# The end of a transformer kernel: the last tile of the last output product, the final norm and the stores in halves of columns

## What is computed

```python
def swiglu_layer(x, g, w_gate, w_up, w_down):      # the last layer, in short
    h = rms_norm_2(x, g)
    return x + (silu(h @ w_gate) * (h @ w_up)) @ w_down

def rms_norm_2(x, g):
    xf = x.astype(jnp.float32)
    y = xf * lax.rsqrt(jnp.mean(xf * xf, axis=-1, keepdims=True) + NORM_EPS)
    return (y * g.astype(jnp.float32)).astype(x.dtype)

...
    return rms_norm_2(x, final_norm)
```

## Time and profile before

| | before |
|---|---|
| three runs | 3154.92, 3155.46, 3160.68 us (median 3155.46) |
| profiled execution: its time | 3158.48 us |
| profiled execution: span of the trace | 3156.6 us, mean granted TensorE clock 0.991 |
| instructions | 44657 |
| PE busy | 3040.8 us (96%) |
| POOL busy | 2161.4 us (68%) |
| DVE busy | 1291.8 us (41%) |
| ACT busy | 729.7 us (23%) |

### The profile page before, as it was taken

One profiled execution on the slowest core, in us unless ns is written; L12 is line 12 of the kernel. 1 busy time (PEld: TensorE's weight loads), 2 busy tenths in 40 slices (PEclk: granted clock), 3 DMA queues, 4 the chain that ended last, 5 costly groups with the idle time before them and its releaser, 6 DMA issues.

```text
span 3156.6 us, 44657 instructions
## 1 busy us (share of the span) xinstructions
PE 3040.8 (96%) x14210; PEld 2409.9 (76%) x14210; DVE 1291.8 (41%) x2257; ACT 729.7 (23%) x1486; POOL 2161.4 (68%) x3010
## 2 busy tenths in 40 slices
PE   7999999999989999999999799899999999999998
PEld 5667888888767688888887577688887777778886
DVE  5653343222455533543235665522225554441223
ACT  4422111010333211210012544410002443320101
POOL 7456777787864577787887355487778444677875
PEclk9999999999999999999999899999999999999999
DMA  4122223222321222222223121122222112222222
GB/s 178 54 68 87 94 95 112 94 97 96 106 100 62 74 94 100 90 100 95 98 100 110 43 68 64 61 94 93 100 94 99 61 54 74 87 87 100 94 100 87
DMA packets 78366, 281.33 MB, mean 89 GB/s; under 512 B 8576, under 2 KB 9088, under 8 KB 77440
## 3 DMA queue, kind: packets, MB, share of 16 engines
q1 hardware_dynamic: 74752, 265.74, 25.1%
q10 hardware_dynamic: 3456, 13.50, 1.2%
HBM read 277.11 MB, written 2.10 MB: 88 GB/s over the span
## 4 chain that ended last, share of the span: by engine, by line
PE 87%; DVE 7%; ACT 3%; issue 1%; DMA 0%; DVEq 0%; POOL 0%; SPq 0%; ACTq 0%; POOLq 0%
PE pa L680 42%; PE pd L680 37%; PE pd L938 2%; PE po L966 2%; ACT work L192 1%; PE pa L946 1%; PE pd L758 1%; DVE h_lo L204 1%; DVE work L200 1%; ACT h_hi L192 1%; DVE po L196 1%; PE pa L723 1%; DVE x_res L196 1%; PE pd L987 1%; DVE qk L204 1%
## 5 line engine op out<-in xcount | busy, mean ns | idle before, releaser
L634 POOL TENSOR_TENSOR w_lo<-w_raw,w_hi 128x256 fp32r<-128x256 f32 x2004 | 1535.9, 797 | 41.8
L629 POOL TENSOR_SCALAR w_hi<-w_raw 128x512 fp32r<-128x512 f32 x1002 | 626.9, 644 | 926.3 <-PE pa L680 557.2
L680 PE MATMUL pa<-h_hi,w_hi 128*128 128x512 f32 (+1 forms) x1944 | 781.6, 402 | 25.1 <-POOL w_lo L634 20.4
L680 PE MATMUL pa<-h_hi,w_lo 128*128 128x512 f32 (+1 forms) x1944 | 752.7, 387 | 0.0
L680 PE MATMUL pa<-h_lo,w_hi 128*128 128x512 f32 (+1 forms) x1944 | 752.4, 387 | 0.0
L680 PEld LDWEIGHTS pa<-h_hi,w_hi 128*128 128x128 f32 x1944 | 366.6, 189 | 136.0 <-issue 55.7
L680 PEld LDWEIGHTS pa<-h_lo,w_hi 128*128 128x128 f32 x1944 | 366.9, 189 | 81.9 <-issue 11.3
L680 PEld LDWEIGHTS pa<-h_hi,w_lo 128*128 128x128 f32 x1944 | 366.4, 188 | 75.5
L680 PE MATMUL pd<-b_hi,w_hi 128*128 128x512 f32 x992 | 389.5, 393 | 6.5 <-DVE x_res L196 2.6
L680 PE MATMUL pd<-b_hi,w_lo 128*128 128x512 f32 x992 | 386.9, 390 | 0.0
L680 PE MATMUL pd<-b_lo,w_hi 128*128 128x512 f32 x992 | 386.9, 390 | 0.0
(11 more groups left out here) (200 smaller groups left out, 3181.0 us busy)
## 6 DMA issues: line engine op xcount, KB each, us to landing
w_raw<-in_w SPq DMA_DIRECT2D x501, 512.0 KB, 3.2
mrg<-in_nabias ACTq DMA_DIRECT2D x2, 2048.0 KB, 9.0
mrg<-in_mem ACTq DMA_DIRECT2D x3, 1024.0 KB, 4.8
x_res<-in_x SPq DMA_DIRECT2D x8, 256.0 KB, 4.9
out_y<-mrg ACTq DMA_DIRECT2D x8, 256.0 KB, 2.1
vbuf<-in_count ACTq DMA_DIRECT2D x2, 512.0 KB, 4.2
qk<-in_mem ACTq DMA_DIRECT2D x1, 1024.0 KB, 7.8
b_all<-in_delta ACTq DMA_DIRECT2D x2, 448.0 KB, 4.0
```

The lines of the kernel that those rows point to most:

```text
L629: ins = nc.gpsimd.tensor_scalar(w_hi[:, j, half], raw[:, j % RR, half], 1.0, 1.0, ALU.mult, ALU.mult)
L634: ins = nc.gpsimd.tensor_tensor(w_lo[:, j, part], raw[:, j % RR, part], w_hi[:, j, part].bitcast(F32), ALU.subtract)
L680: ins = mm(out, a, b, start=(first and k == 0 and e == 0), stop=(last and k == k_n - 1 and e == 2))
```

## The change

The last group's output product gets functions of its own, `last_residual` on PE, ACT and DVE. Tiles 0 to 6 are made as before in 512 columns, written out instead of looped over. Tile 7 is made in two halves of 256 columns, each in a bank of its own, and all that follows goes by these halves: addition, square, product with ones (`last_sum`), logarithm, exponential, square, the two root steps, scaling and stores. The sum of the first half stands in PE's list before the last two of the second half's six steps. ACT multiplies tiles 0 to 2 by the gain ahead of time (`gained`), POOL multiplies these by `rx`, DVE scales tiles 3 to 7. SP stores the first halves of all tiles and the second halves of POOL's, ACT the second halves of DVE's.

```diff
@@ @block.sync
+            def store(k, h, scaled, count):
+                sp.wait_ge(scaled, count)
+                sp.dma_start(dram["out"][k][:, HALVES[h]], mrg[:, k, HALVES[h]]).then_inc(out_first, 16)
+
+            for at in range(KT - POOLED):
+                store(POOLED + at, 0, last_root, 2 + at)
+            for k in range(POOLED):
+                store(k, 0, by_pool, 1 + k)
+            for k in range(POOLED):
+                store(k, 1, by_pool, 1 + POOLED + k)
+            sp.wait_ge(out_first, 16 * (KT + POOLED))
@@ @block.gpsimd
+            pool.wait_ge(gained, POOLED)
+            for h, half in enumerate(HALVES):
+                pool.wait_ge(last_root, 1 + h * (1 + KT - POOLED))
+                for k in range(POOLED):
+                    nc.gpsimd.tensor_tensor(mrg[:, k, half], mrg[:, k, half], rx[:, half], ALU.mult).then_inc(by_pool, 1)
@@ @block.tensor
+            def last_residual(k_n):
+
+                pe.wait_ge(split_full, n.last("split_full"))
+                for m in range(KT - 1):
+                    linear(bank_d(), B, k_n).then_inc(cdone, 1)
+                s = next_chunk()
+                for h, half in enumerate(HALVES):
+                    bank = bank_d()
+
+                    def waits(k):
+                        if h and k == k_n - 2:
+                            last_sum(0)
+                    ins = products(bank[:, 0:S // 2], [w_tile(s, k) for k in range(k_n)],
+                                   [act_tile(B, k, half) for k in range(k_n)], waits=waits)
+                    if h:
+                        ins.then_inc(cdone, 1)
+                    else:
+                        n.take("pd_full")
+                        ins.then_inc(pd_full, 1)
+                last_sum(1)
+
+            def last_sum(h):
+                bank, half = bank_a(), HALVES[h]
+                if h == 0:
+                    pe.wait_ge(acc_part, n.at("acc_part", n.n["acc_part"] + KT - 2))
+                mm(bank[:, 0:S // 2], ones, acc[:, half], start=True, stop=False)
+                pe.wait_ge(last_squared, h + 1)
+                mm(bank[:, 0:S // 2], ones, pair2[:, 1, half], start=False, stop=True).then_inc(last_summed, 1)
...
-                    residual(B, g, ends and not last)
                     if ends and last:
-                        for _ in range(KT):
-                            n.take("acc_part")
+                        last_residual(g)
+                    else:
+                        residual(B, g, ends)
...
-            stream_norm(True)
@@ @block.scalar
+            def last_residual():
+                for m in range(KT - 1):
+                    n.take("x_full")
+                    prepare(m)
+                    if m < POOLED:
+                        f(mrg[:, m], x[:, m], ACT.Copy, scale=col("final", m)).then_inc(gained, 1)
+                act.wait_ge(acc_part, n.free("acc_part", n.n["acc_part"], 2))
+                for h, half in enumerate(HALVES):
+                    act.wait_ge(last_added, h + 1)
+                    f(pair2[:, 1, half], x[:, KT - 1, half], ACT.Square).then_inc(last_squared, 1)
+                    act.wait_ge(last_summed, h + 1)
+                    mean_square = pa[n.take("pa_done") % RA][:, 0:S // 2]
+                    chain(f(rx[:, half], mean_square, ACT.Ln, scale=1.0 / D))
+                    chain(f(rx[:, half], rx[:, half], ACT.Exp, scale=-0.5))
+                    f(pair2[:, 1, half], rx[:, half], ACT.Square).then_inc(last_rooted, 1)
...
-            stream_norm()
-            for k in range(KT):
-                act.wait_ge(t_full, n.at("t_full", n.take("t_full")))
-                act.dma_start(dram["out"][k], mrg[:, k]).then_inc(out_in, 16)
-            act.wait_ge(out_in, 16 * KT)
+            for at in range(KT - POOLED):
+                k = POOLED + at
+                act.wait_ge(last_root, 1 + KT - POOLED + 2 + at)
+                act.dma_start(dram["out"][k][:, HALVES[1]], mrg[:, k, HALVES[1]]).then_inc(out_in, 16)
+            act.wait_ge(out_in, 16 * (KT - POOLED))
@@ @block.vector
+            def last_residual():
+                clear_sum()
+                for m in range(KT - 1):
+                    add_x(m)
+                    prepare(m, "final", False)
+                for h, half in enumerate(HALVES):
+                    if h:
+                        n.take("cdone")
+                    d = full_d(h == 1)
+                    v.tensor_tensor(x[:, KT - 1, half], x[:, KT - 1, half], pd[d % RD][:, 0:S // 2], ALU.add)\
+                        .then_inc(last_added, 1)
+                dve.wait_ge(last_added, 2)
+                for h, half in enumerate(HALVES):
+                    mean_square = pa[n.take("pa_done") % RA][:, 0:S // 2]
+                    dve.wait_ge(last_rooted, h + 1)
+                    chain(v.scalar_tensor_tensor(pair2[:, 0, half], mean_square, -0.5 / D, pair2[:, 1, half],
+                                                 ALU.mult, ALU.mult))
+                    v.scalar_tensor_tensor(rx[:, half], pair2[:, 0, half], 1.5, rx[:, half], ALU.add, ALU.mult)\
+                        .then_inc(last_root, 1)
+                    dve.wait_ge(last_root, 1 + h * (1 + KT - POOLED))
+                    for k in range(POOLED, KT):
+                        scaled(mrg[:, k, half], x[:, k, half], col("final", k), rx[:, half]).then_inc(last_root, 1)
...
-            stream_norm()
-            for k in range(KT):
-                n.take("t_full")
-                scaled(mrg[:, k], x[:, k], col("final", k), rx[:, :]).then_inc(t_full, 1)
```

More of the change, by code:

```diff
@@ L555, in build @@
         set_up = sem("set_up")
+        last_added, last_squared = sem("last_tile_added"), sem("last_tile_squared")
+        last_summed, last_rooted, last_root = sem("last_half_summed"), sem("last_half_rooted"), sem("last_root")
+        gained, by_pool = sem("gained"), sem("scaled_by_pool")
+        out_first = sem("first_halves_stored")
+        HALVES = (slice(0, S // 2), slice(S // 2, S))
+        POOLED = 3
         block = ctx.enter_context(nc.Block())
@@ L1538, in residual, with ffn @@
                     prepare(m, name)
-            def ffn(next_name=None, between=None):
+            def last_residual():
[13 more added lines that the diff above has]
+                    f(pair2[:, 1, half], rx[:, half], ACT.Square).then_inc(last_rooted, 1)
+            def ffn(next_name=None, between=None, last=False):
                 stream_norm()
@@ L1559, in ffn @@
                         log_and_exp()
-                    residual(ends, next_name)
+                    if ends and last:
+                        last_residual()
+                    else:
+                        residual(ends, next_name)
             def gates(l):
@@ L1689, in cross_and_ffn @@
                 half_residual(f"b{l}_ffn")
-                ffn(None if l else "b1_mix")
+                ffn(None if l else "b1_mix", last=l == 1)
             load(tabs[:], dram["tabs"][:, 0:512], aux_in[5])
@@ L2171, in add_x, with residual @@
                 v.give(x_full)
-            def residual(name=None, split=True):
+            def last_residual():
[20 more added lines that the diff above has]
+                        scaled(mrg[:, k, half], x[:, k, half], col("final", k), rx[:, half]).then_inc(last_root, 1)
+            def residual(name=None):
                 if name:
@@ L2177, in residual @@
                         add_x(m)
-                        prepare(m, name, split)
+                        prepare(m, name)
                     return
@@ L2222, in ffn @@
                         between(number)
-                    residual(next_name if number == len(GROUPS) - 1 else None, next_name != "final")
+                    if number == len(GROUPS) - 1 and next_name == "final":
+                        last_residual()
+                    else:
+                        residual(next_name if number == len(GROUPS) - 1 else None)
             def gates(l):
```

## The result

| | before | after |
|---|---|---|
| median (22 executions each) | 3156.44 us | 3161.57 us |
| lowest to highest | 3154.92 to 3160.68 | 3158.77 to 3164.20 |
| profiled execution: time / span | 3158.48 / 3156.6 us | 3161.30 / 3159.5 us |
| mean granted TensorE clock | 0.991 | 0.989 |

The ratio after by before is 1.0015, with a 95% interval of [1.0009, 1.0022], +5.1 us in the medians. That is within 0.2%, but the interval leaves no change out: the kernel is a little slower. In microseconds it goes from +2.8 to +6.9. The forecast was +3.1 us and 3158.6 us, its range ended at 3162.3.

The account below looks back on a forecast made before the run. PE was taken to bound the kernel, with a 14.95 us serial tail behind its last product. Base 3155.46 us plus 3.4 (late start), plus 1.6 (clock), less 1.85 (tail), +3.1 in all, gave 3158.6 us; range 3155.0 to 3162.3.

Parts of the forecast that it names:

- late start of tile 0: Start of the last output product: tile 0 waits for all six hidden tiles, so its sixth step comes later, +3.4 us.
- low clock behind the stand: Behind PE's 3.85 us stand ahead of tile 0: one 3.4 us stretch at clock 0.50, +1.6 us, bounds 0 and 5.
- writing the loop out: Tiles 0 to 6 of the last output product: same 126 matmuls at the same pace, no cost.
- tail in halves: From tile 7 to the end: halves scaled on two engines end at 3154.75 instead of 3156.6, -1.85 us.
- Rival (2): Behind the stand ahead of tile 0: the clock stays up or falls while PE still stands, 3157.0 us; chance 0.2.
- Rival (3): Scalings in the tail: no collision on SBUF, both engines at their own pace, 1.8 us less, 3156.8 us; chance 0.1.
- Rival (4): Last output product: the late start costs nothing, only the shorter tail shows, 3153.6 us; chance 0.06.
- rival (5): Behind the stand ahead of tile 0: the low clock stays, costing 5 us, 3162.0 us; chance 0.1.
- 3.45 us for a half: Tail: POOL's three scalings take 2.5 us, DVE makes 3.15 tiles meanwhile and 1.85 alone in 0.95.
- scalings at 0.7 to 0.8 us each: Sign in the changed kernel's profile: DVE's `mrg` scalings take this long beside POOL's.
- The store: End of the tail: last store taken as 2.44 us as before; an estimate of 0.3 us shorter was left out.

Follow-up runs that it names:

- e3_fill: The changed kernel with 15 filler matmuls, results unused, ahead of its late wait: 3159.34 us, ratio to before 1.0009.
- e1_early: The changed kernel with the waits of before at tile 0, the last hidden tile awaited only ahead of the sixth step: 3156.58 us, ratio to before 1.0000.
- e2_wait: The kernel before, with only the last output product's wait for all six hidden tiles moved ahead of tile 0: 3162.11 us, ratio to before 1.0017.
- e6_root_psum: e1_early, but ACT copies the root into PSUM and DVE reads it there from its second tile on: 3153.61 us, ratio to before 0.9992.
- e4_dve_all: e1_early with DVE scaling all eight tiles in halves and POOL none: 3155.45 us, ratio to before 0.9997.
- e5: e1_early with POOL scaling four tiles instead of three and DVE four: 3155.61 us, ratio to before 0.9993.
- e7_gain_ahead: e6_root_psum with ACT multiplying seven tiles by the gain ahead of time instead of three: 3153.96 us, ratio to before 0.9990.
- e8_fill6: e3_fill with 6 filler matmuls instead of 15 ahead of the late wait, one execution: 3158.18 us.

## Why the prediction was right, and where its sum was off

The forecast was +3.1 us, within 0.2%, by a late tile 0 and one stretch of low clock, less a shorter tail. All three parts are there, and the sign is right. Of the parts:

| term | forecast | measured |
|---|---|---|
| late start of tile 0 | +3.4 | +3.41 (e3_fill against e1_early) |
| low clock behind the stand | +1.6 | +1.6 (changed kernel against e3_fill; e2_wait) |
| writing the loop out | 0 | 0 (e1_early: 25.29 us as before) |
| tail in halves | -1.85 | -1.1 |
| sum | +3.1 | +3.9 by the traces, +5.1 by the medians |

The measured median, 3161.57, lies 3.0 us above the forecast 3158.6 and only 0.7 below the end of the range. One microsecond of the three is the base: the forecast started from the median of three runs, 3155.46, and that of 22 is 3156.44. The tail's term makes 0.8, and 1.2 are open (below). That the range held is in part luck, since its upper end was set for a clock that stays low, which did not happen. Two slips in the working change nothing that matters: the two root steps of 0.43 us end at 3144.26 by the sum, not at 3144.32, and (2) less the 1.8 us of (3) is 3155.2, not 3155.0.

**The wait.** It was read from one row, the 0.45 us stand ahead of the sixth step: five steps lay in front of a wait that was always going to be waited for, and moving them behind it costs their full length, because PE has no later stand that could take it up. Rival (4), that the late start costs nothing, is refuted by e2_wait.

**The clock.** The value between the two bounds, 0 and 5 us, was the right one: one stretch at the low level, then back. Rival (2) would have given 3112.20 to 3115.50 at 1.00, as e3_fill has it, and rival (5) a clock that stays down past 3115.6. The two neighbours that it was placed between, stands of 3.27 and 4.21 us, were a good guide: in all eleven traces the clock is low behind these two (0.50 to 0.68 in the 3.3 us that follow). The third, the stand of 2.34 us that kept the clock and carried rival (2), was a poor one: in two of the eleven traces, that of the changed kernel among them, the clock falls behind it too (last section).

**The tail.** Here a size was off, the term "3.45 us for a half". The path of the first half up to the first scaling was forecast at 3144.42 - 3137.40 = 7.02 us and took 3148.58 - 3141.37 = 7.21 (+0.2). The five scalings took 3.81 and 3.73 us instead of 3.45 twice (+0.64), the step from one series to the next 3153.58 - 3152.39 = 1.19 instead of 0.99 (+0.2), and the last store 2.2 instead of 2.44 (-0.25). These give +0.8, the difference between -1.85 and -1.1. The greatest part is the collision: beside POOL DVE needs 0.84 us and 1.05 for the first, not the 0.79 of the earlier trace rows, and what POOL holds up is three DVE instructions, 2.8 us, as the third goes on when POOL's 2.5 us have ended. The sign that the prediction gave, scalings at 0.7 to 0.8 us each, was so far too low. Rival (3), no collision, is refuted, and it names what could be had: e6_root_psum takes most of the collision away and wins 0.9 us.

**The store.** The prediction left out that a half tile's store is shorter. It is, by some 0.25 us (2.2 against 2.44). The estimate that the prediction worked out from the Trainium skill, "DMA: Bandwidth & Descriptors", section "Anatomy of one DMA — SWDGE (gpsimd) path", was 0.3 less; the trace comes near it, though the page's figures are for transfers that GpSimd issues, and these are issued by ACT and SP.

**What stays open.** The medians rose by 5.1 us, the parts add up to 3.9. The interval of the ratio, +2.8 to +6.9 us, holds both 3.9 and the forecast's 3.1. The difference of 1.2 shows again between e1_early and before, equal in the medians while the tail is 1.1 us shorter in the trace; the interval there is 2.8 us to either side. In e4_dve_all and e6_root_psum it goes the other way: the medians lie 1.1 and 3.1 us below before, the tails only 0.3 and 2.0. So scatter can explain it. Some of the scatter goes with the clock: of the 27 executions of before on the chip of e5 to e7, the 12 with a mean granted clock of 0.990 took 3158.4 us on average, the 15 with more took 3156.2. Whether a small cost of the new kernels ahead of the last output product is hidden in it was not settled: the traces reach the last `up` matmul at times from 3103.75 to 3108.04 us whatever the change.

## What to carry to other kernels

When a loop is written out by hand, put its waits beside those of the loop that it replaces: a wait for "all" in front of a product costs every step that could have run under it, here 3.4 us, and the stand that it makes can cost clock on top, here 1.6 us, which is more than the whole new tail gave back. Work that is given to a second engine is worth what the two do together: DVE lost 1.2 of the 1.55 us that POOL took off it, until one of DVE's operands lay in PSUM. And once the compute part of a tail is short, look at the spacing of the last stores.

## What the runs showed of the hardware that was not expected

- The length of the last stand alone doesn't decide whether the clock falls behind it. At some 1809 us, in code that no experiment touches, PE stands for 2.31 to 2.35 us in all eleven traces. In nine of them the clock is 1.00 in the 3.3 us that follow, before among them; in e3_fill and in the changed kernel it is not. At 887 us the clock falls behind a stand of 2.29 us in the trace of before, and stays up behind one of 2.53 us in e4_dve_all. Each pair of rows is PE's first instruction behind the stand and the stretch there, of the changed kernel, of before and of e4_dve_all:

```profile
1808.99 0.79 PE L703 MATMUL pa<-h_hi,w_hi 128*128 128x512 f32 x1 [2.31 <-DVE mrg L196]
...
1808.99:1812.29 3.30, 3.30 (x8) 2.65 (x9) 1.94 (x10) 1.95 (x7) 0.00 (x0) 0.53 0.42 159
```

```profile
886.90 0.58 PE L680 MATMUL pa<-b_hi,w_hi 128*128 128x256 f32 x1 [2.29 <-DVE rope L204]
...
886.70:890.00 3.30, 3.10 (x14) 3.10 (x15) 3.01 (x5) 0.22 (x1) 3.22 (x5) 0.50 0.11 24
```

```profile
887.61 0.39 PE L702 MATMUL pa<-b_hi,w_hi 128*128 128x256 f32 x1 [2.53 <-DVE rope L204]
...
887.61:890.91 3.30, 3.30 (x26) 3.17 (x28) 2.88 (x5) 0.02 (x1) 3.22 (x5) 1.00 0.46 159
```

  So behind a stand of 2.3 to 2.5 us one trace doesn't tell what the next execution will do, and e8_fill6's fall behind 2.45 us is such a case. Behind those of 3.27 us and more that are named in this text the clock was low in every trace.
- A DVE instruction that reads two tiles from SBUF beside POOL takes 0.84 us, but the first of a series 0.97 to 1.05; in e7_gain_ahead a first TENSOR_TENSOR that started 0.05 us ahead of POOL's took 0.43 us, and one that started 0.03 us behind it 0.98. In e6_root_psum a first SCALAR_TENSOR_TENSOR that started 0.04 us ahead took 1.04 all the same. What decides it was not looked into.
- A 128 KB store of half a tile takes 1.7 to 1.8 us from issue to landing in the median, where the 256 KB one of before took 2.1: half the bytes save 0.3 to 0.4 us. In e7_gain_ahead the median over all stores is 1.9, the longest 2.5.
